# Splitting the embedding projection of an encoder layer between its two norms, with its squares summed by GpSimd

## What is computed

```python
h  = layer_norm(ALPHA * x + merged @ w_o[i], ln1_g[i], ln1_b[i])          # first norm
g_, u_ = jnp.split(h @ w_gate_up[i], 2, axis=-1)
h2 = layer_norm(ALPHA * h + (silu(g_) * u_) @ w_down[i], ln2_g[i], ln2_b[i])  # second norm
e  = rms_norm(p[i] @ w_ple[i], ple_norm_g[i])     # p[i]: 512 x 256, w_ple[i]: 256 x 1024
x  = h2 + e * sigmoid(h2 @ w_ple_gate[i])
```

## Time and profile before

| | us |
|---|---|
| median of 3 runs | 2415.36 |
| lowest and highest | 2410.65, 2415.5 |
| the profiled execution | 2412.09 |
| its span (first to last instruction) | 2410.5 |

### The profile page before, as it was taken

One profiled execution on the slowest core, in us unless ns is written; L12 is line 12 of the kernel. 1 busy time (PEld: TensorE's weight loads), 2 busy tenths in 40 slices (PEclk: granted clock), 3 DMA queues, 4 the chain that ended last, 5 costly groups with the idle time before them and its releaser, 6 DMA issues.

```text
span 2410.5 us, 35334 instructions
## 1 busy us (share of the span) xinstructions
PE 2369.6 (98%) x11464; PEld 1946.8 (81%) x11464; DVE 1510.7 (63%) x2553; ACT 1371.2 (57%) x2242; POOL 581.7 (24%) x721
## 2 busy tenths in 40 slices
PE   8999999999999999999999999999999999999998
PEld 6878788887877788888788787888878778888876
DVE  5999999999546211113768999999995461111136
ACT  6756656475564644345557466664756656443455
POOL 3423333242111111111124243332421111111110
PEclk9999999999999999999999999999999999999999
DMA  8576585766888789889665857757577868988995
GB/s 213 130 168 147 130 181 112 173 136 153 182 183 194 163 191 194 192 191 214 167 148 120 183 123 159 169 106 174 123 174 175 194 164 186 196 189 194 194 213 139
DMA packets 111173, 406.04 MB, mean 168 GB/s; under 512 B 12337, under 2 KB 12337, under 8 KB 110769
## 3 DMA queue, kind: packets, MB, share of 16 engines
q0 software_dynamic: 54144, 197.16, 49.1%
q1 hardware_dynamic: 55728, 202.66, 25.3%
q10 hardware_dynamic: 1152, 4.37, 0.5%
HBM read 402.04 MB, written 2.10 MB: 168 GB/s over the span
## 4 chain that ended last, share of the span: by engine, by line
PE 88%; DVE 5%; ACT 2%; issue 2%; DMA 2%; POOL 0%; ACTq 0%; POOLq 0%; SPq 0%; DVEq 0%
PE bank L855 24%; PE bank L857 23%; PE bank L856 23%; PE bank L897 3%; PE bank L898 3%; PE bank L900 2%; PE bank L971 2%; DMA w_lo<-w_stream 2%; PE bank L977 1%; PE bank L959 1%; PE bank L1186 1%; PE bank L942 1%; PE bank L943 1%; PE bank L927 1%; PE bank L988 1%
## 5 line engine op out<-in xcount | busy, mean ns | idle before, releaser
L354 POOL DMA_DIRECT2D w_lo<-w_stream x376 | 328.6, 874 | 1594.0 <-ACT w_lo L467 1539.4
L855 PE MATMUL bank<-x_hi,w_hi 128*128 128x512 f32 x1728 | 686.7, 397 | 0.0
L857 PE MATMUL bank<-x_hi,w_lo 128*128 128x512 f32 x1728 | 674.0, 390 | 0.0
L856 PE MATMUL bank<-x_lo,w_hi 128*128 128x512 f32 x1728 | 673.3, 390 | 0.0
L466 ACT ACTIVATE w_hi<-w_raw 128x1024 fp32r<-128x1024 f32 x378 | 403.2, 1067 | 279.9 <-PE bank L857 239.8
L467 ACT ACTIVATE w_lo<-w_raw 128x1024 fp32r<-128x1024 f32 x378 | 400.3, 1059 | 0.0
L855 PEld LDWEIGHTS bank<-x_hi,w_hi 128*128 128x128 f32 x1728 | 324.6, 188 | 68.8 <-issue 3.4
L857 PEld LDWEIGHTS bank<-x_hi,w_lo 128*128 128x128 f32 x1728 | 324.5, 188 | 68.9
L856 PEld LDWEIGHTS bank<-x_lo,w_hi 128*128 128x128 f32 x1728 | 324.8, 188 | 67.9 <-issue 3.3
L1268 DVE SCALAR_TENSOR_TENSOR z_a<-glu_out,params,z_a 128x497 f32<-128x497 f32 (+14 forms) x480 | 321.2, 737 | 0.0
L1726 DVE TENSOR_TENSOR glu_out<-bank,sigmoids 128x512 f32<-128x512 f32 x44 | 30.4, 692 | 416.5 <-PE bank L857 416.5
(11 more groups left out here) (245 smaller groups left out, 3662.8 us busy)
## 6 DMA issues: line engine op xcount, KB each, us to landing
w_raw<-w_stream SPq DMA_DIRECT2D x378, 512.0 KB, 5.0
w_lo<-w_stream POOLq DMA_DIRECT2D x376, 512.0 KB, 7.5
z_b<-x_in SPq DMA_DIRECT2D x4, 512.0 KB, 7.1
w_ple_in<-w_ple ACTq DMA_DIRECT2D x2, 1024.0 KB, 11.5
out<-z_b SPq DMA_DIRECT2D x4, 512.0 KB, 5.0
ple_p<-p_in ACTq DMA_DIRECT2D x2, 512.0 KB, 6.5
params<-par_in ACTq DMA_DIRECT2D x2, 340.0 KB, 3.9
tmp_m<-w_dt ACTq DMA_DIRECT2D x2, 256.0 KB, 5.0
```

The costliest lines, as they stand in the source:

```text
L354: gp.dma_start(wlo[:, s, :], w_stream[cyc, s].bitcast(F32R), accum_op=ALU.add).then_inc(lo_done[s], 16)
L855: pe.matmul(dst, wh, mh, start=first, stop=False)
L856: pe.matmul(dst, wh, ml, start=False, stop=False)
L857: return pe.matmul(dst, wl, mh, start=False, stop=last)
```

## The change

It does six things, in both layers.

1. The projections 4 to 7 move from the first norm to the second. They take their own copy of `p` (`ple_p_again`) and the second half of `w_ple` (`w_ple_rest`), both loaded in the third down stage behind the load of the step weights; at the first norm only the first half of `w_ple` is loaded. Each of the eight has a fixed bank.
2. After the first norm the gate/up phase starts with two slots side by side (`together=2`).
3. ACT squares tiles 0 to 3 where it squared all eight, and evacuates and squares tiles 4 to 7 between the rounding steps of the second norm.
4. POOL adds the eight tiles of squares into the first (`add_e_squares`, seven adds of 128x512 in place): three between the second and third `lo` of the second `C_DOWN2` cycle, four before the last `lo` of the first `C_PLE` cycle.
5. PE runs one product with `mean1` for eight, behind the first two slots of the gate stage, once the adds are done.
6. ACT takes the root after its last `hi` of the first gate cycle and the split of the step weights, and loads the sigmoid's table right behind it (`want(2, ...)`). DVE splits the step weights first, waits for the root, and scales the tiles of `ge` two ahead of their use instead of all at once.

```diff
-E_BANKS = (6, 7, 1, 2, 3)
+E_BANKS = (6, 7, 2, 3, 6, 2, 3, 7)
+EARLY_E = KT // 2
...
+            def add_e_squares(L, tiles):
+                for m in tiles:
+                    gp.wait_ge(esq_ready, seen(KT * L + m + 1))
+                    gp.wait_ge(e_summed, seen((KT - 1) * L + m - 1))
+                    settle(gp)
+                    gp.tensor_tensor(esq[:, 0, :], esq[:, 0, :], esq[:, m, :], ALU.add).then_inc(e_summed, 1)
...
-                with gp.Fori(C_GATE_A, CYCLES - 1) as c:
+                with gp.Fori(C_GATE_A, C_DOWN2) as c:
                     lo(base + c + 1, 0, 1, 2, 3)
+                lo(base + C_DOWN2 + 1, 0, 1)
+                add_e_squares(L, range(1, EARLY_E))
+                lo(base + C_DOWN2 + 1, 2, 3)
+                lo(base + C_PLE, 0, 1, 2)
+                add_e_squares(L, range(EARLY_E, KT))
+                lo(base + C_PLE, 3)
+                lo(base + C_PLE + 1, 0, 1, 2, 3)
...
-                act.dma_start(wpl[:, :, :], w_ple[L]).then_inc(ple_loaded, 16)
+                act.dma_start(wpl[:, :, :], w_ple[L, :, :, 0:D // 2]).then_inc(ple_loaded, 16)
...
-                norm_round(k, 0, za, xh, O_LN1)
-                for m in range(1, KT - 1):
+                for m in range(KT):
                     norm_round(k, m, za, xh, O_LN1)
-                    ple(m + 1)
-                norm_round(k, KT - 1, za, xh, O_LN1)
+                    if 0 < m < EARLY_E - 1:
+                        ple(m + 1)
                 hi(on(post, C_UP0), SLOTS - 1)
...
                 act.dma_start(tmf, w_dt[L + 1]).then_inc(dtw_loaded, 16)
-                for m in range(KT):
+                act.dma_start(pin_b[:, :, :], p_in[L]).then_inc(p_loaded, 16)
+                act.dma_start(wpl_b[:, :, :], w_ple[L, :, :, D // 2:]).then_inc(ple_loaded, 16)
+                for m in range(EARLY_E):
+                    e_square(m)
...
+                ple(4)
                 token_std(n, k)
                 diagonal(n)
-                for m in range(KT):
-                    norm_round(k, m, zb, aah, O_LN2)
-                    if m == 4:
-                        act.wait_ge(esq_used, seen(L + 1))
-                        act.activation(erms[:, :], bank[6][:, :], ACT.Sqrt, bias=eps[:, 1:2]).then_inc(estd_ready, 1)
+                ple(5)
+                norm_round(k, 0, zb, aah, O_LN2)
+                e_square(4)
+                norm_round(k, 1, zb, aah, O_LN2)
+                ple(6)
+                norm_round(k, 2, zb, aah, O_LN2)
+                e_square(5)
+                norm_round(k, 3, zb, aah, O_LN2)
+                ple(7)
+                norm_round(k, 4, zb, aah, O_LN2)
+                e_square(6)
+                norm_round(k, 5, zb, aah, O_LN2)
+                e_square(7)
+                norm_round(k, 6, zb, aah, O_LN2)
+                norm_round(k, 7, zb, aah, O_LN2)
                 hi(on(post, C_PLE), SLOTS - 1)
                 act.wait_ge(dtw_loaded, 16 * (L + 2))
                 act.activation(dwh[:, :], tmf, ACT.Copy).then_inc(dtw_hi, 1)
+                act.wait_ge(esq_used, seen(L + 1))
+                act.activation(erms[:, :], bank[6][:, :], ACT.Sqrt, bias=eps[:, 1:2]).then_inc(estd_ready, 1)
+                want(2, ACT.Sigmoid)
...
-                for m in range(2, KT):
+                for m in range(2, EARLY_E):
                     ple(m)
                 phase(post, C_UP0, C_DOWN0, xh, xl, ready=lambda m: pe.wait_ge(xl_done, seen(KT * (k + 1) + m + 1)),
-                      held=lambda: pe.wait_ge(e_evac, seen(KT * (L + 1))))
+                      together=2, held=lambda: pe.wait_ge(e_evac, seen(KT * L + EARLY_E)))
...
+                def e_mean_square():
+                    pe.wait_ge(e_evac, seen(KT * (L + 1)))
+                    pe.wait_ge(e_summed, seen((KT - 1) * (L + 1)))
+                    pe.matmul(bank[6][:, :], mean1[:, :], esq[:, 0, :], start=True, stop=True).then_inc(esq_used, 1)
...
-                e_mean_square(range(2))
+                ple(4)
                 offset_and_sums(k + 2, 2 * L + 1)
-                e_mean_square(range(2, 4))
+                ple(5)
                 spread_rstd(2 * L + 1)
-                e_mean_square(range(4, KT))
+                ple(6)
+                ple(7)
                 phase(post, C_PLE, CYCLES, aah, aal, ready=lambda m: pe.wait_ge(xl_done, seen(KT * (k + 2) + m + 1)),
-                      together=2)
+                      together=2, held=e_mean_square)
...
+                dve.wait_ge(dtw_hi, seen(L + 2))
+                rest(dwl[:, :], tmf, dwh[:, :], dtw_lo)
                 dve.wait_ge(estd_ready, seen(L + 1))
                 step(dve.reciprocal(erms[:, :], erms[:, :]))
+                e_normed(0)
+                e_normed(1)
...
                 for m in range(KT):
+                    if m + 2 < KT:
+                        e_normed(m + 2)
+                    dve.wait_ge(en_ready, seen(n + 1))
```

More of the change, by code:

```diff
@@ L1757, in _, with e_normed @@
                 summed_norm(NORMS * L + LN_2, 2 * L + 1, post + C_DOWN2, zb, aah, aal, xl_done, O_LN2, 1.0)
-                dve.wait_ge(estd_ready, seen(L + 1))
-                step(dve.reciprocal(erms[:, :], erms[:, :]))
-                dve.wait_ge(dve_order, issued())
-                for m in range(KT):
+                def e_normed(m):
                     dve.scalar_tensor_tensor(out=ge[:, m, :], in0=ge[:, m, :], scalar=par[:, O_PLE + m:O_PLE + m + 1],
@@ L1766, in _ @@
                 rest(dwl[:, :], tmf, dwh[:, :], dtw_lo)
-                dve.wait_ge(en_ready, seen(KT * (L + 1)))
+                dve.wait_ge(estd_ready, seen(L + 1))
+                step(dve.reciprocal(erms[:, :], erms[:, :]))
+                dve.wait_ge(dve_order, issued())
                 restart()
+                e_normed(0)
+                e_normed(1)
                 for m in range(KT):
                     s, n = m % SLOTS, KT * L + m
+                    if m + 2 < KT:
+                        e_normed(m + 2)
+                    dve.wait_ge(en_ready, seen(n + 1))
                     dve.wait_ge(evac[s], seen(post + C_PLE + m // SLOTS + 1))
```

40 lines of the change are left out of this document (21 added, 19 removed).

## The result

| | us |
|---|---|
| before, median of 7 runs | 2412.64 (2410.65 to 2415.5) |
| changed kernel, median of 7 runs | 2422.71 (2418.39 to 2424.91) |
| ratio | 1.0041, 95% interval 1.0031 to 1.0052 |
| profiled executions, before and after | 2412.09 and 2422.71 (spans 2410.5 and 2421.1) |

The changed kernel is slower by 10 us, 0.41%, more than the 0.2% that a measurement can tell. The forecast was a change of +1.6 us. The time lies in the forecast's range (2405 to 2427), but not where most of its chance lay: no measurable change had been given 0.51, slower 0.27.

The account below looks back on a forecast made before the run. PE's order of work was taken to bound the kernel, with late weight tiles next. Terms -4.8 + 1.8 + 2 x (1.5 + 0.8) = +1.6 us on 2415.36 gave 2417.0 us, range 2405 to 2427.

Parts of the forecast that it names:

- PE bounds the kernel: Whole kernel: PE holds 88% of the chain; a shorter list of products helps only where nothing else is late next.
- First norm, -4.8 us: First norm: four projections leave PE, 6.9 us a layer; slot 0's weight tile lets 2.4 through, -4.8 us over both layers.
- Two slots together cost nothing: Gate/up start behind the first norm: with two slots PE takes 1.37 us a tile, never catches DVE up, costs nothing.
- Third down stage, +1.8 us: Third down stage: second loads and three adds make weight tiles late, +1.8 us, between -1.2 and +6.
- rival C: Third down stage: the transfers take the full +6, total +5.8, 2421.2 us; chance 0.13.
- rival B: Second norm: the adds hold DVE, 4.4 us a layer, total +8.8, 2424.2 us; sign low parts over 0.9 us; chance 0.19.
- The Trainium skill's add: POOL's adds: 2048 f32 take 4497 ns on the skill's page, so one of 512 about 1.1 us; forecast took 1.2.
- Second norm, +1.5 a layer for the chain: Second norm: ACT waits for the one product, so the last cycle's slot 0 lands late; +1.5 us a layer, up to +2.7.
- The adds beside DVE, +0.8 a layer: Second norm: four POOL adds hold up DVE's low parts, +0.8 us a layer; zero to 1.6.
- Sum: Whole kernel: -4.8 + 1.8 + 2 x (1.5 + 0.8) = +1.6 us.
- Rival A: Whole kernel: the work leaves PE for good, 12 us less, 2403.4 us; chance 0.25.
- The base: Starting time: the forecast added +1.6 us to a median of 2415.36 us, giving 2417.0.

Follow-up runs that it names:

- e4_bias_later: Changed kernel with the eight z_a offset steps on ACT put between the steps of the first gate/up cycle instead of ahead of it; 2412.39 us, ratio 0.9996.
- e7_one_slot: Changed kernel with one slot at a time behind the first norm (together=2 taken back); 2419.83 us, ratio 1.0031.
- e5_hi_first: Changed kernel with `hi` of the last cycle's slot 0 put ahead of ACT's wait for the sum of squares; 2417.32 us, ratio 1.0015.
- e6_no_late_adds: Changed kernel without POOL's four late adds, the mean of squares taken over tiles 0 to 3 alone; 2420.77 us, ratio 1.0028.
- e9_all: Changed kernel with the edits of e8_early_place, e4_bias_later and e5_hi_first together; 2403.95 us, ratio 0.9960.
- e2_adds_late: Changed kernel with POOL's three early adds moved behind the transfers of the third down stage, together with the four late ones; 2423.53 us, ratio 1.0047.
- e3_both_moved: Changed kernel with the edits of e8_early_place and e2_adds_late together; 2420.68 us, ratio 1.0029.
- e8_early_place: Changed kernel with the second loads of p and w_ple moved to the start of the third gate and up stage; 2420.0 us, ratio 1.0026.

## Why the prediction was right in its mechanisms and short in its sum

- **PE bounds the kernel; what is late next decides.** Right: each place named had its wait. The granted clock, which the forecast read as 0.9 or more in every slice, had no term in its sum; a fall of it behind a new wait was put at nothing without a reason.
- **First norm, -4.8 us.** The step was right. "Waits for `w_lo` of some 4.4 us before slot 3 and slot 0" measured 0.82 + 2.85 = 3.67, and 0.52 + 3.95 = 4.47 in layer 1. Slot 0 begins 2.7 and 1.95 us earlier against the spreading product (2.4 forecast). e4_bias_later shows the cause by taking it away. What the step lacked is the price of the wait itself: behind the longer one the clock gave layer 1's gain back, and the two stretches brought -1.9 instead of -4.8. Without the 3.4 us lost there at the lower clock they would have brought -5.3.
- **Two slots together cost nothing.** Right in time, but it also brought nothing (e7_one_slot), and it gathered PE's waits into long ones, in the profiled executions.
- **Third down stage, +1.8 us.** This is the term that was most mis-sized: +7.3 measured, above the end of +6 that rival C stood for. C's 2421.2 (chance 0.13) is 1.5 us off the measured time, as is B's 2424.2 (0.19). The landing of 9.8 us was right (10.2 and 9.7). Wrong were three sizes behind it: an add took 1.54 us and not 1.2, and the third transfer left 10.7 us into the stage (1133.26 - 1122.55) where the forecast had 9.2 (1136.2 - 1127.0); it took 9.5 us to land and not 7.5, so that PE waited 4.26 us and not 1.4; and the clock added 1.7 us. That the loads are the cause is shown by the six kernels without them in this stage; of the adds, that they hold the third transfer back some 1.8 us is shown (5.65 against 3.82 behind the second), what that costs PE is not.
- **The Trainium skill's add.** The estimate from its page "GPSIMD Engine Reference", section "3.1 Elementwise — side-by-side cycle accounting", was 1.1 us; the 14 adds here took 1.30 to 1.63.
- **Second norm, +1.5 a layer for the chain.** The mechanism and its place are shown by e5_hi_first, 1.7 and 2.1 us. The product stands 1176.30 - 1159.48 = 16.8 us behind the spreading product; the forecast's 1172.7 was 15.3 behind the one at 1157.36. The 1.5 more are late low parts.
- **The adds beside DVE, +0.8 a layer.** Short: 1.9 and 2.6 us by e6_no_late_adds. Low parts of 1.11 and 1.76 us beside adds of 1.5 are rival B's sign ("over 0.9 us"), but B's size of 4.4 a layer did not come; the low parts lost 0.37 + 1.02 + 0.38 + about 1.0 = 2.8 us. The trace agrees with the Trainium skill, page "SBUF — State Buffer", section "Who interferes with whom", that DVE steps with both tensors in SBUF are held up beside POOL; steps of DVE that read an accumulator kept their 0.74 us. The steps with both tensors in SBUF lost 0.37 (1.11 for 0.74) to 1.70 us (2.38 for 0.68), a part of the add or the whole of it; the whole, by that rule, made the term 1.6, nearer to the measured 1.9 and 2.6 than the 0.8 I took.
- **Sum.** Forecast -4.8 + 1.8 + 4.6 = +1.6. Measured -1.9 + 7.3 + 7.0 = +12.4, and -1.8 in stretches that the change does not touch; 5.1 of the 12.4 are the clock. Rival A, the whole gain of PE, was wrong for this kernel, but with ACT reordered the first norms gave nearly that (-11.7 in e4_bias_later and -12.1 in e9_all, of the 13.7 that the forecast named as this term's end).
- **The base.** The forecast's 2417.0 stood on a median of three, 2415.36. By the seven runs known since (2412.64) it would have been 2414.2, so the true miss is 8.5 us, and part of the nearness of 2417.0 to 2422.71 is luck. That the time still lies in the range is owed to the range's width of 22 us, which took in rivals B and C.

**What stays open.** The size of the third down stage's loss. Kernels with the loads and the adds in this stage had +6.6 and +0.8, +2.2 and -0.2, +4.4 and +2.8, +1.2 and +0.7, +7.1 and +0.1 (changed, e7, e4, e5, e6). Part of the scatter is the clock (1.7 us each in changed and e6, layer 0, and in both layers of e4). The rest goes with the landing of the third transfer: PE waited 4.26 and 4.00 us where it took 9.5 and 9.6 us, 2.30 where it took 8.9, and at most 1.2 in the other seven layers, where it took 5.9 to 7.7. The landing times differ from execution to execution, and I have no run that says what sets them. At the second norms 0.7 to 1.2 us remain with all repairs (e9_all); of this no run tells the adds from the evacuations. And no run says why the clock falls behind one wait and not behind another of the same length.

## What to carry to other kernels

Work taken off the bounding engine is worth no more than the slack of the next thing that it waits for; find that chain (here ACT's steps in front of the next weight tile) and move what is not urgent behind it in the same edit. Put extra loads where the next tiles are not already landing late, and judge a part such as "two slots together" only with its neighbours in place: it was worth nothing in one setting and 2.8 us a layer in another. And count a wait of the bounding engine at more than its length: one of 3.95 us was followed here by 3.4 us lost to the clock.

## What the runs showed of the hardware that I had not expected

**A wait of PE of a few microseconds can cost as much again through the clock, in a stream that is busy otherwise.** In the stages that the change touches PE had 17 waits of 2.3 to 4.3 us in all these kernels. In or within 1.2 us behind thirteen of them the granted clock fell to the lower level, 1.2 GHz. By the granted clock over 20 us around the wait: 0.83 after 4.18 us (e2_adds_late), 3.91 (e5_hi_first), 3.70 (e3_both_moved) and 3.19 (e6_no_late_adds), as after 3.95 in the changed kernel; 0.91 after 4.21 (e5_hi_first), 4.00 (e6_no_late_adds), 3.83 and 2.57 (e3_both_moved), 3.42 (e8_early_place), 2.77 that followed one of 1.41 (e2_adds_late) and 2.30 (e4_bias_later), as after 4.26 in the changed kernel. There was no fall after 2.38 (e7_one_slot), 2.85 (changed), 3.03 (e6_no_late_adds) and 3.50 (e8_early_place). So the length alone does not decide. A figure of 0.91 over 20 us is 1.7 to 1.8 us lost, one of 0.83 is 3.4. The kernel before has such falls too, four of 20 us at 0.91 in its scan, each behind a wait of some 1.45 us, of which it has seven there, and in e4_bias_later one in the third down stage came 2.4 us behind a wait of 1.44. So this is not the change's alone; but none of the falls of the kernel before lies in the stages here.
